# Decoder step on one core: gated unit on rounded operands, cross output's first two groups one after the other, selector products on rounded rows

## What is computed

```python
y = jax.nn.gelu(y)                          # end of the S5 branch, width 512
y = y * jax.nn.sigmoid(y @ w_glu)           # gated unit
w_intra = where(mask, b[i] - b[j] + li[j], -inf)          # mLSTM, per head
s = einsum('bhid,bhjd->bhij', q, k) * exp(w_intra - m_tok)
merged = sigmoid(za)*(y_a@w_branch_a) + sigmoid(zb)*(y_b@w_branch_b) + sigmoid(zc)*(y_c@w_branch_c)
x = x + cross_attn(...)                     # ends in o @ w_o
```

## Time and profile before

| | |
|---|---|
| median of 3 runs | 2369.13 us (2362.12 to 2372.32) |
| the profiled execution | 2369.92 us, span 2367.3 us |
| PE busy | 2260.8 us (95%) |
| DVE busy | 1145.2 us (48%) |
| ACT busy | 597.0 us (25%) |
| POOL busy | 281.7 us (12%) |
| mean granted PE clock | 0.98 of full |

### The profile page before, as it was taken

One profiled execution on the slowest core, in us unless ns is written; L12 is line 12 of the kernel. 1 busy time (PEld: TensorE's weight loads), 2 busy tenths in 40 slices (PEclk: granted clock), 3 DMA queues, 4 the chain that ended last, 5 costly groups with the idle time before them and its releaser, 6 DMA issues.

```text
span 2367.3 us, 34371 instructions
## 1 busy us (share of the span) xinstructions
PE 2260.8 (95%) x14712; PEld 2177.6 (92%) x14712; DVE 1145.2 (48%) x1264; ACT 597.0 (25%) x740; POOL 281.7 (12%) x436
## 2 busy tenths in 40 slices
PE   5799989999999999999999999999999999999995
PEld 5699978888989999999999998999999999999995
DVE  4716533334444344323654222437566655556665
ACT  4422233222322222233332124222111111111112
POOL 5989700000000000000000000000000000000000
PEclk9899999999989999999999999999999999999998
DMA  6311123121322222224322143111111111111111
GB/s 234 107 45 48 51 92 109 55 72 73 126 101 82 79 77 88 105 81 191 134 99 88 45 169 143 36 46 54 45 46 48 51 46 45 46 45 46 54 40 72
DMA packets 45221, 190.36 MB, mean 80 GB/s; under 512 B 5136, under 2 KB 5200, under 8 KB 41488
## 3 DMA queue, kind: packets, MB, share of 16 engines
q1 hardware_dynamic: 32112, 117.13, 14.4%
q0 software_dynamic: 11104, 54.41, 6.1%
q10 hardware_dynamic: 1872, 16.83, 1.8%
HBM read 152.59 MB, written 35.93 MB: 80 GB/s over the span
## 4 chain that ended last, share of the span: by engine, by line
PE 88%; issue 4%; DVE 3%; ACT 2%; POOL 1%; DMA 1%; DVEq 0%; ACTq 0%; POOLq 0%
PE ps L256 24%; PE ps L257 24%; PE ps L259 24%; PE ps L1715 1%; PE ps L1006 1%; PE ps L2043 1%; PE ps L2067 1%; DVE GT L399 1%; PE ps L371 1%; PE ps L372 1%; PE ps L374 1%; PE ps L2077 1%; POOL W L660 1%; PE ps L1691 0%; DVE WL L250 0%
## 5 line engine op out<-in xcount | busy, mean ns | idle before, releaser
L256 PE MATMUL ps<-XH,WH 128*128 128x344 f32 x1656 | 536.5, 327 | 8.5 <-DVE WL L250 6.0
L257 PE MATMUL ps<-XL,WH 128*128 128x344 f32 x1512 | 481.4, 322 | 0.0
L256 PE MATMUL ps<-XN,WH 128*128 128x344 f32 x1248 | 399.2, 322 | 4.3 <-issue 4.1
L257 PE MATMUL ps<-XN,WH 128*128 128x344 f32 x1248 | 397.2, 322 | 0.0
L250 DVE TENSOR_TENSOR WL<-WRAW,WH 128x1024 fp32r<-128x1024 f32 x175 | 220.3, 1260 | 309.3 <-ACT WH L245 308.2
L259 PE MATMUL ps<-XH,WL 128*128 128x344 f32 x1656 | 353.2, 322 | 0.0
L256 PEld LDWEIGHTS ps<-XH,WH 128*128 128x128 f32 x1656 | 314.8, 190 | 19.7 <-issue 14.4
L245 ACT ACTIVATE WH<-WRAW 128x1024 fp32r<-128x1024 f32 x175 | 184.3, 1054 | 534.6 <-PE ps L259 522.5
L257 PEld LDWEIGHTS ps<-XL,WH 128*128 128x128 f32 x1512 | 286.8, 190 | 0.2
L259 PEld LDWEIGHTS ps<-XH,WL 128*128 128x128 f32 x1656 | 279.4, 190 | 0.0
L259 PE MATMUL ps<-XN,WL 128*128 128x344 f32 x1248 | 264.3, 320 | 0.0
(11 more groups left out here) (512 smaller groups left out, 3165.9 us busy)
## 6 DMA issues: line engine op xcount, KB each, us to landing
WRAW<-in_wslabs SPq DMA_DIRECT2D x175, 512.0 KB, 3.5
scratch_spill<-STAGE SPq DMA_DIRECT2D x40, 516.0 KB, 2.6
ZS<-scratch_spill POOLq DMA_DIRECT2D x24, 516.0 KB, 5.5
XIN<-in_xT POOLq DMA_DIRECT2D x1, 4128.0 KB, 18.4
XR<-in_xT ACTq DMA_DIRECT2D x2, 2064.0 KB, 8.7
out_y<-XR SPq DMA_DIRECT2D x8, 516.0 KB, 3.0
CACHES<-in_ck ACTq DMA_DIRECT2D x4, 1024.0 KB, 14.2
CACHES<-in_cv ACTq DMA_DIRECT2D x4, 1024.0 KB, 15.6
```

The costliest lines, as they stand in the source:

```text
L256: pe.matmul(out[t], WH[:, slot, w, :], xh(k, t), start=(k == 0), stop=False)
L257: pe.matmul(out[t], WH[:, slot, w, :], xl(k, t), start=False, stop=False)
```

## The change

Four things. (1) The gated unit's weights enter the slab stream as two slabs (SL_GLU), and its products become split steps on SUH and SUL, the rounded and remaining parts of the gelu result; gelu of tiles 0 to 2 moves into the S5 stage; the first two output groups run block by block, as the input blocks arrive; the result is written over SUT, so the load of MQT now waits for its store, and the wait for that store is gone from ACT. The last fill group's emptying stands behind the first rounding on ACT. (2) The rows of the mLSTM are split into rounded rows ROWR (high parts in rows 0 to 3 and 64 to 67, remainders in 32 to 35 and 96 to 99), and a selector PICK with ones at both rows replaces `spread`; identity and mask are copied to fp32r tiles. (3) The first two tiles of the S5 result are split after the first SL_GR group, none after the fourth. (4) `pe_start`, until now written out in `pe_out`, does the cross output's first two groups in turn.

```diff
 SL_SU = 17
-SL_MQ, SL_MV = 21, 29
-SL_GQ, SL_GKV = 33, 35
-SL_MO = 41
-SL_Z = 45
-SL_GR = 69
-SL_GATE = 73
+SL_MQ, SL_GLU, SL_MV = 21, 29, 31
+SL_GQ, SL_GKV = 35, 37
+SL_MO = 43
+SL_Z = 47
+SL_GR = 71
+SL_GATE = 75
...
 NRM = cst("NRM", [128, 16])
+UNIT, MASKR = cst("UNIT", [128, 128], F32R), cst("MASKR", [128, 128], F32R)
+PICK = cst("PICK", [128, 8], F32R)
...
         dve_lo(dve, n0 + count + 1, (n0 + count - 1) % 2)
+def pe_start(pe, n0, g0, ks, xl):
+    for s in range(2):
+        n, g = n0 + s, g0 + s
+        pe.wait_ge(w_lo, n + 1)
+        pe.wait_ge(acc_free[g % 2], g // 2)
+        for k in range(KT):
+            if s == 0:
+                pe.wait_ge(xl_ready, KT * ks + k + 1)
+            last = split_step(pe, banks(g % 2), n % 2, xh_cols, xl, k, k, KT)
+        last.then_inc(acc_ready, 1)
 def pe_first(pe, n0, g0, ks, xl=None):
...
-    for m in range(2):
-        pool.dma_start(WPL[:, m], I["wplain"][m]).then_inc(wp_loaded[m], 16)
     pool.wait_ge(s5_done, 4)
     pool.dma_start(O["s5_state"], SOUT[:]).then_inc(s5_stored, 16)
     pool.wait_ge(fl_stored, 16 * 8)
...
 def act_s5(act):
     for q in range(4):
...
         act_fill(act, f"s{q}d")
+        if q:
+            act.wait_ge(s5_done, q)
+            nc.scalar.activation(SUT[:, q - 1, :], SUT[:, q - 1, :], ACT.Gelu_apprx_tanh).then_inc(glu_in, 1)
         act.wait_ge(s5_pe, s5_at("tt", q + 1))
         nc.scalar.activation(TT[:, :, :].rearrange("p g (t c) -> p t g c", c=16),
...
                                              in1=ps[:, 5 + k, :].rearrange("p (t n) -> p t n", n=128),
                                              op0=M, op1=AD))
-        dve_fill(dve, f"s{q}g")
         dve.wait_ge(s5_pe, s5_at("yst", q + 1))
         v = SUT[:, q, T:N]
         nc.vector.scalar_tensor_tensor(out=v, in0=v, scalar=S5D[:, q:q + 1], in1=ps[:, 7, 0:8],
                                        op0=M, op1=AD).then_inc(s5_done, 1)
+        if q < 3:
+            dve_fill(dve, f"s{q}g")
 def pe_s5(pe):
     evacuated(pe, G_SU + 4)
...
-YC = area("YC", [128, 4, N], 8256)
+SUH, SUL = area("SUH", [128, 4, N], 4 * N, F32R), area("SUL", [128, 4, N], 8 * N, F32R)
 glu_in, glu_sig, glu_out, yc_stored = sem("glu_in"), sem("glu_sig"), sem("glu_out"), sem("yc_stored")
-def plain_product(pe, n, g, slot, gslot, rhs):
-    pe.wait_ge(wp_loaded[slot], n)
-    pe.wait_ge(acc_free[gslot], g // 2)
-    for k in range(4):
-        for t in range(NTG):
-            last = pe.matmul(banks(gslot)[t], WPL[:, slot, k, :], rhs(k, t), start=(k == 0), stop=(k == 3))
-    last.then_inc(acc_ready, 1)
+glu_hi, glu_lo = sem("glu_hi"), sem("glu_lo")
 def pe_glu(pe):
     pe.wait_ge(fl_free, 8)
-    pe.wait_ge(s5_done, 4)
-    pe.wait_ge(glu_in, 4)
-    for m in range(4):
-        plain_product(pe, 16 * (m // 2 + 1), GR_GLU + m, m % 2, (GR_GLU + m) % 2,
-                      lambda k, t: SUT[:, k, t * TG:(t + 1) * TG])
+    def step(m, k):
+        return split_step(pe, banks((GR_GLU + m) % 2), (SL_GLU + m // 2) % 2,
+                          lambda k, t: SUH[:, k, t * TG:(t + 1) * TG],
+                          lambda k, t: SUL[:, k, t * TG:(t + 1) * TG], 4 * (m % 2) + k, k, 4)
+    pe.wait_ge(w_lo, SL_GLU + 1)
+    for k in range(4):
+        pe.wait_ge(glu_lo, k + 1)
+        for m in range(2):
+            last = step(m, k)
+            if k == 3:
+                last.then_inc(acc_ready, 1)
+    pe.wait_ge(w_lo, SL_GLU + 2)
+    for m in range(2, 4):
+        pe.wait_ge(acc_free[(GR_GLU + m) % 2], (GR_GLU + m) // 2)
+        for k in range(4):
+            last = step(m, k)
+        last.then_inc(acc_ready, 1)
 def act_glu(act):
+    def hi(q):
+        nc.scalar.activation(SUH[:, q, :], SUT[:, q, :], ACT.Copy).then_inc(glu_hi, 1)
     act.wait_ge(s5_done, 4)
-    for q in range(4):
-        nc.scalar.activation(SUT[:, q, :], SUT[:, q, :], ACT.Gelu_apprx_tanh).then_inc(glu_in, 1)
+    act.wait_ge(glu_in, 3)
+    hi(0)
+    act_fill(act, "s3g")
+    hi(1)
+    hi(2)
+    nc.scalar.activation(SUT[:, 3, :], SUT[:, 3, :], ACT.Gelu_apprx_tanh).then_inc(glu_in, 1)
+    act.wait_ge(glu_in, 4)
+    hi(3)
     for m in range(4):
         act.wait_ge(acc_ready, GR_GLU + m + 1)
         if m >= 2:
             act.wait_ge(glu_out, m - 1)
         nc.scalar.activation(t3(TMP[:, m % 2, :]), acc((GR_GLU + m) % 2), ACT.Sigmoid).then_inc(glu_sig, 1)
+        if m % 2:
+            act_hi(act, None, (SL_GLU + m // 2) % 2, 16 * ((SL_GLU + m // 2) // 2 + 2), None)
+def dve_glu_lo(dve):
+    for q in range(4):
+        dve.wait_ge(glu_hi, q + 1)
+        nc.vector.tensor_tensor(SUL[:, q, :], SUT[:, q, :], SUH[:, q, :].bitcast(F32),
+                                ALU.subtract).then_inc(glu_lo, 1)
+        if q == 0:
+            dve_fill(dve, "s3g")
 def dve_glu(dve):
+    dve.wait_ge(glu_in, 4)
     for m in range(4):
         dve.wait_ge(glu_sig, m + 1)
         dve.sem_inc(acc_free[(GR_GLU + m) % 2], 1)
-        nc.vector.tensor_tensor(YC[:, m, :], SUT[:, m, :], TMP[:, m % 2, :], ALU.mult).then_inc(glu_out, 1)
+        nc.vector.tensor_tensor(SUT[:, m, :], SUT[:, m, :], TMP[:, m % 2, :], ALU.mult).then_inc(glu_out, 1)
+        if m % 2:
+            dve_lo(dve, SL_GLU + m // 2 + 2, (SL_GLU + m // 2) % 2)
 def pool_glu(pool):
-    for m in range(2, 4):
-        pool.wait_ge(acc_ready, GR_GLU + m - 1)
-        pool.dma_start(WPL[:, m % 2], I["wplain"][m]).then_inc(wp_loaded[m % 2], 16)
+    pool.wait_ge(acc_ready, GR_GLU + 4)
+    pool.dma_start(MKT, I["spill"][4:8].rearrange("h p n -> p h n")).then_inc(mk_in, 16)
 def pool_store_yc(pool):
     pool.wait_ge(glu_out, 4)
-    pool.dma_start(I["yc"], YC[:]).then_inc(yc_stored, 16)
+    pool.dma_start(I["yc"], SUT).then_inc(yc_stored, 16)
+    pool.wait_ge(yc_stored, 16)
     pool.dma_start(MQT, I["spill"][0:4].rearrange("h p n -> p h n")).then_inc(mq_in, 16)
...
     return ps[:, (5, 3)[c // 4] + c % 4 // 2, (c % 2) * 256:(c % 2) * 256 + 129]
+ROWR = at("ROWR", [128, T], O_TMP + N * 4, F32R)
+def picked(k):
+    return PICK[:, k:k + 1].to_broadcast([128, 128])
...
-    act.wait_ge(yc_stored, 16)
     act_project(act, SL_MV, G_MV, 2, MK, 4)
     act.wait_ge(ml_e, 1)
...
+    act.wait_ge(ml_rows, 1)
+    nc.scalar.activation(ROWR[64:68, :], ROWS[64:68, 0:T], ACT.Copy).then_inc(ml_rows, 1)
     act_project(act, SL_MV + 2, G_MV + 2, 2, MK, 6)
     for h in range(4):
...
     tt(ROWS[0:4, 0:T], b[:, 0:T], m[:, 0:T], SU_)
+    L(nc.vector.memset(ROWR[:, :].bitcast(F32), 0.0))
+    L(nc.vector.tensor_copy(ROWR[0:4, :], ROWS[0:4, 0:T]))
+    tt(ROWR[32:36, :], ROWS[0:4, 0:T], ROWR[0:4, :].bitcast(F32), SU_)
+    L(nc.vector.tensor_copy(UNIT[:, :], IDENT))
+    L(nc.vector.tensor_copy(MASKR[:, :], MASKNEG))
+    tt(PICK[:, 0:4], IDENT[:, 0:4], IDENT[:, 32:36], AD)
+    tt(PICK[:, 4:8], IDENT[:, 64:68], IDENT[:, 96:100], AD)
     tt(R[1][:, 0:T], li[:, 0:T], b[:, 0:T], SU_)
     c8 = lambda x: x.rearrange("p (c i) -> p c i", i=128)
     ends = lambda x: c8(x[:, 0:T])[:, :, 127]
...
     dve_project(dve, SL_MV + 2, 2)
+    dve.wait_ge(ml_rows, 8)
+    tt(ROWR[96:100, :], ROWS[64:68, 0:T], ROWR[64:68, :].bitcast(F32), SU_)
     dve.wait_ge(ml_ej, 1)
     L(nc.vector.tensor_copy(BCOL[:, :, :], ps[:, 7, 64:96].rearrange("p (c h) -> p c h", h=4)))
...
         for k in range(2):
-            pe.matmul(ps[:, 3 + k, :], spread(h), ROWS[:, 512 * k:512 * k + 512], start=True, stop=False)
-            pe.matmul(ps[:, 3 + k, :].rearrange("p (c i) -> p c i", i=128), IDENT,
-                      MASKNEG.unsqueeze(1).to_broadcast([128, 4, 128]), start=False, stop=True)
+            pe.matmul(ps[:, 3 + k, :], picked(h), ROWR[:, 512 * k:512 * k + 512], start=True, stop=False)
+            pe.matmul(ps[:, 3 + k, :].rearrange("p (c i) -> p c i", i=128), UNIT[:, :],
+                      MASKR[:, :].unsqueeze(1).to_broadcast([128, 4, 128]), start=False, stop=True)
         pe.wait_ge(ml_dve, ml_did("ke", h + 1))
         for c in range(NCH):
             last = pe.matmul(two(5)[:, c, :], MKT[:, h, chunk(c)], MQT[:, h, chunk(c)], start=True, stop=True)
...
         for k in range(2):
-            last = pe.matmul(ps[:, 3 + k, :], spread(64 + h), ROWS[:, 512 * k:512 * k + 512], start=True, stop=True)
+            last = pe.matmul(ps[:, 3 + k, :], picked(4 + h), ROWR[:, 512 * k:512 * k + 512], start=True, stop=True)
         last.then_inc(ml_pe, 1)
         pe.wait_ge(ml_dve, ml_did("st", h + 1))
         for c in range(4):
...
         if m == 0:
             act.wait_ge(yc_in, 16)
-        act_part_hi(act, 0, (m,))
+        act_part_hi(act, 0, ((0, 1), (2,), (3,), ())[m])
 def dve_gr(dve):
     for m in range(4):
         gr_dve(dve, m)
-        dve_part_lo(dve, 0, (m,))
+        dve_part_lo(dve, 0, ((0, 1), (2,), (3,), ())[m])
 def act_gates(act):
     act.wait_ge(ml_y, 8)
...
 def pe_out(pe):
-    for s in range(2):
-        n, g = SL_OUT + s, G_OUT + s
-        pe.wait_ge(w_lo, n + 1)
-        pe.wait_ge(acc_free[g % 2], g // 2)
-        for k in range(KT):
-            if s == 0:
```

(20 more changed lines are left out.)

## The result

The changed kernel takes 2354.6 us, the median of 12 runs (2349.0 to 2361.7); the kernel before took 2371.9 us in the runs beside it. The ratio is 0.9938 (95% interval 0.9926 to 0.9950), a gain of 17.3 us where 35.2 were forecast. The profiled execution is the longest of the twelve, 2361.7 us with a span of 2359.9. PE is still the engine of the chain.

What follows compares the result with a forecast made beforehand. PE, busy 95% of the span, was taken to bound the kernel, with gaps costing idle time and half clock. Gains of 7.6, 15.0, 7.4 and 6.4 less 1.2 us made 35.2, so 2335 us, range 2327 to 2350.

Steps and rivals of the forecast that it cites:

- Sum.: Whole kernel: 7.6 + 15.0 - 1.2 + 7.4 + 6.4 = 35.2 us off the profiled execution's 2369.9 us, giving 2334.7.
- Part 1, the gated unit: Gated unit: rounded steps and a shorter idle start on PE gain 7.6 us, or 10.6 at full clock.
- MQT: Ahead of the heads: its load, expected 24 us after the unit's end, lands late and PE stops; 2393 us, chance 0.01.
- The gelus in S5: S5 stage: gelus of 1.0 us each on ACT, beside PE's fill steps and product runs, cost nothing.
- Part 2, the selectors: mLSTM heads: six rounded selector products cost 1.4 us instead of 5.15 per head, gaining 15.0 us over four heads.
- The ECOL wait: Ahead of the mLSTM heads: one more DVE subtraction lengthens PE's wait, a loss of 1.2 us.
- Part 3, the branch gates: Ahead of the branch gates: the wait on YLC and the half clock behind it vanish, gaining 7.4 us.
- Part 4, the cross output: Cross output: groups in turn remove a 3.8 us wait and the half clock behind it, gaining 6.4 us.
- a clock that stays up at the unit: Rival at the gated unit: the clock does not fall after the shortened gap; time 2332 us, chance 0.25.
- Selectors: Rival in the heads: selector products keep the plain price or the time returns as a wait; 2350 us, chance 0.09.
- roundings: Rival at gated unit and cross output: ACT and DVE fall behind, both gains are lost; 2349 us, chance 0.06.

Runs made afterwards that it cites:

- before_pad45: The kernel before with 45 more do-nothing instructions on PE ahead of the first PA transposes, putting its loop where the change puts it: 2390.9 us, ratio 1.0093.
- sel_plain: The changed kernel with the six selector products of a head back in plain arithmetic, 48 more instructions on PE: 2346.2 us.
- gates_back: after_pad48 with the last tile of YLC split behind the fourth projection again, as before the change: 2340.9 us.
- co_back: after_pad48 with the cross output's first two groups in step again, as before the change: 2337.6 us.
- after_again: The changed kernel, unpadded and unaltered, in a second profiled execution: span 2350.7 us.
- after_pad16: The changed kernel with 16 more do-nothing instructions on PE ahead of the first PA transposes: 2326.3 us, ratio 0.9824.
- after_pad48: The changed kernel with 48 more do-nothing instructions on PE ahead of the first PA transposes: 2330.0 us, ratio 0.9836.
- before_pad61: The kernel before with 61 more do-nothing instructions on PE, its loop at the same place as in after_pad16: 2367.0 us, ratio 0.9984.
- before_pad24: The kernel before with 24 more do-nothing instructions on PE ahead of the first PA transposes: 2377.9 us, ratio 1.0034.

## Why the prediction was wrong

**The step that failed** is "Sum." It takes the four parts off the time of the profiled execution and so takes every other stage at its former length; no term, no rival and no bound dealt with PE's own instruction stream. The change added 45 instructions ahead of the feed-forward loop. That put the loop's head among the last instructions of a fetched packet. The four jumps back cost 3.9 us of idling instead of 1.0, and half clock behind each: 20.9 us in before_pad45 against before. This is about the missing amount, 35.2 minus 17.3 or 17.9 us, and the two measurements of the change at equal places (36.3 and 40.7 us) show that nothing else of that size is missing. The row of 4.1 us "issue" stood in the same list as the earlier trace rows, and 1.1 us on ECOL was taken from there while it was passed over.

The other steps, against what was measured:

- **Part 1, the gated unit, 7.6 us.** First product 2.84 us after the last transpose (2.9 forecast), next projection 28.3 us after it (26 to 29 forecast, 36.5 before). Whether the clock falls was indeed open. Of the ten profiled executions with the new unit and the gelus in S5 (after twice, the padded ones, sel_plain, gates_back, co_back), two show no half-clock stretch here, six one of 3.4 us and two one of 6.8. The forecast had taken 6.8. To the end of the projections' wait on MKV the gain is 8.4 us with a stretch of 6.8 (after), 9.5 with one of 3.4 (after_again) and 10.9 with none (after_pad16, after_pad48). The forecast had 7.6 and, at full clock, 10.6. MQT caused no wait. The gelus in S5 were taken at nothing; the stage is some 2 us longer, and its cause stays open.
- **Part 2, the selectors, 15.0 us.** Neighbouring heads lie 39.79 us apart on average instead of 43.55, 3.76 each and 15.0 in all; 16.1 us by sel_plain. The ECOL wait grew by 1.4 us (1.2 forecast).
- **Part 3, the branch gates, 7.4 us.** 6.9 and 7.5 us in the two executions of after, 8.3 by gates_back.
- **Part 4, the cross output, 6.4 us.** 6.2 us as the stage of before_pad61 against after_pad16, 5.4 to 7.5 by co_back.
- **The rivals.** None of them explains the time. The first, a clock that stays up at the unit, came about in two of ten executions and is worth 2 to 3 us, in the other direction. Selectors, roundings and MQT behaved as in the forecast.

The four parts gave 36 to 41 us with the loop at equal places; from the total of 17 alone one might have concluded that half of them had been hidden by other work.

**The better version.** after_pad12, the changed kernel with 12 instructions that do nothing, takes 2326.6 us, 28 us below the changed kernel and 43 us below the one before (its ratio to the kernel before is 0.9824, and the interval lies wholly below the changed kernel's). after_pad4 has the same effect with 4 but sits right behind the edge.

## What to carry to other kernels

A long unrolled loop can have a price at every jump back, here from nothing to some 6.5 us (26 us over four jumps, before_pad45 against before_pad61), which depends on where it begins in its engine's instruction stream. Any edit ahead of it changes that, even one that shares nothing with it. So count the instructions that an edit adds to the busiest engine ahead of such a loop, look for "issue" waits at the loop's head and at the packets of the instruction queue, and compare two versions only with the loop at the same place. Here places 256 instructions apart were alike. If the loop nearly fits in what the engine keeps, some padding in an idle place can be worth more than the edit itself.

## What the runs showed of the hardware

- 45 instructions that do nothing made this kernel 20 us slower, and 4 of them made the changed one 27 us faster.
- PE keeps this loop of 1,764 instructions (just under seven packets of 16,384 bytes) over all its passes if it lies well in the packets: 76 instruction packets instead of 112, and 530 us without a gap. At the places of before, before_pad24 and after it fetches nine packets in each pass, mostly hidden, but for what stands right behind the jump.
- Gaps of 3.7 to 4.4 us ahead of the loop's first product were followed by half clock every time, eight times in the two executions of after and four times in before_pad45; the pairs of gaps of up to 1.2 us in before_pad24, 3 us apart, never were. The gap of 2.84 us ahead of the gated unit was followed by half clock in eight of ten executions.
- Waits that are already fulfilled aren't free: between 109 instructions of two waits (8.1 us of issue) and 272 (25.9 us) each more costs 0.11 us.
